# Splitting one weight load of a streamed expert layer into five transfers

## The reference

```
def _expert_choice_ffn(h, w_router, w_gate, w_up, w_down):
    ...
    def expert(args):
        xe, wg, wu, wd = args
        a = jnp.einsum('bcd,df->bcf', xe, wg)
        u = jnp.einsum('bcd,df->bcf', xe, wu)
        return jnp.einsum('bcf,fd->bcd', jax.nn.silu(a) * u, wd)

    out = lax.map(expert, (xin, w_gate, w_up, w_down))
    out = out * g[..., None].astype(out.dtype)
    return jnp.zeros_like(h).at[bi, idx].add(out)
```

## Time and profile before

| | |
|---|---|
| median of three runs | 1815.48 us (1813.34 to 1815.5) |
| the profiled execution, its own time | 1813.51 us |
| its span | 1811.5 us |
| TensorE busy | 1350.9 us, 75% of the span |
| VectorE, ScalarE, GpSimd busy | 438.3, 143.5, 36.2 us |
| moved by DMA | 629.34 MB, mean 347 GB/s |
| chain that ended last | DMA 57%, TensorE 40% |

### The profile page before, as it was taken

One profiled execution on the slowest core, in us unless ns is written; L12 is line 12 of the kernel. 1 busy time (PEld: TensorE's weight loads), 2 busy tenths in 40 slices (PEclk: granted clock), 3 DMA queues, 4 the chain that ended last, 5 costly groups with the idle time before them and its releaser, 6 DMA issues.

```text
span 1811.5 us, 22396 instructions
## 1 busy us (share of the span) xinstructions
PE 1350.9 (75%) x10436; PEld 750.2 (41%) x10436; DVE 438.3 (24%) x681; ACT 143.5 (8%) x316; POOL 36.2 (2%) x54
## 2 busy tenths in 40 slices
PE   9999999999999765756656575666656574665665
PEld 7888588848765331312312231322222131221321
DVE  3553333368655101010211101010210101021111
ACT  3200021132221000000000000000000000000001
POOL 1001010000000000000000000000000000000000
PEclk9999999999999877878777877878777887778788
DMA  7425372432399999999999999999999999999996
GB/s 253 141 95 157 101 251 94 148 139 94 132 383 414 432 431 432 433 432 432 432 431 431 433 434 432 431 430 432 435 431 433 431 430 433 433 430 434 431 428 274
DMA packets 50688, 629.34 MB, mean 347 GB/s; under 512 B 3098, under 2 KB 4293, under 8 KB 36772
## 3 DMA queue, kind: packets, MB, share of 16 engines
q1 hardware_dynamic: 47776, 620.01, 81.5%
q0 software_dynamic: 2400, 7.56, 1.5%
q10 hardware_dynamic: 420, 0.34, 0.1%
HBM read 626.79 MB, written 1.11 MB: 347 GB/s over the span
## 4 chain that ended last, share of the span: by engine, by line
DMA 57%; PE 40%; DVE 1%; ACT 1%; issue 0%; POOL 0%; DVEq 0%; SPq 0%; ACTq 0%
DMA arena<-in_w_down 21%; DMA arena<-in_w_gate 18%; DMA arena<-in_w_up 18%; PE psum L907 12%; PE psum L1517 7%; PE psum L1573 4%; PE psum L1277 3%; PE psum L1207 2%; PE psum L910 2%; PE psum L1367 1%; PE psum L913 1%; PE psum L1181 1%; PE psum L1195 1%; PE psum L1279 1%; PE psum L1506 1%; PE psum L1426 0%
## 5 line engine op out<-in xcount | busy, mean ns | idle before, releaser
L1517 PE MATMUL psum<-arena 128*32 128x352 f32 x4096 | 409.4, 565 | 326.0 <-DMA arena<-in_w_up 194.7
L1517 PEld LDWEIGHTS psum<-arena 128*32 128x32 f32 x4096 | 150.7, 132 | 585.0 <-issue 223.4
L1573 PE MATMUL psum<-arena 128*32 128x512 f32 x1408 | 232.0, 774 | 62.4 <-DMA arena<-in_w_down 62.4
L907 PE MATMUL psum<-arena 128*128 128x256 f32 x976 | 222.1, 383 | 1.3 <-ACT arena L611 0.7
L907 PEld LDWEIGHTS psum<-arena 128*128 128x128 f32 x976 | 181.7, 189 | 30.1 <-issue 2.2
L2203 DVE TENSOR_SCALAR arena<-arena 128x704 f32<-128x704 f32 x16 | 12.0, 753 | 654.1 <-ACT arena L856 654.0
L1573 PEld LDWEIGHTS psum<-arena 128*32 128x32 f32 x1408 | 62.6, 134 | 218.4 <-issue 138.5
L2210 DVE TENSOR_TENSOR arena<-psum,arena 128x704 f32<-128x704 f32 x16 | 21.5, 1344 | 303.5 <-PE psum L1517 303.5
L1506 PE MATMUL psum<-arena 128*128 128x32 f32 x512 | 89.5, 347 | 0.8 <-DVE arena L2167 0.8
L1506 PEld LDWEIGHTS psum<-arena 128*128 128x128 f32 x512 | 88.7, 273 | 2.1 <-issue 1.1
L859 ACT ACTIVATE arena<-psum 128x1024 f32<-128x1024 f32 x15 | 15.4, 1024 | 778.1 <-PE psum L1573 778.1
(11 more groups left out here) (385 smaller groups left out, 951.9 us busy)
## 6 DMA issues: line engine op xcount, KB each, us to landing
arena<-in_w_gate SPq DMA_DIRECT2D x32, 5632.0 KB, 46.6
arena<-in_w_up SPq DMA_DIRECT2D x31, 5632.0 KB, 45.2
arena<-in_w_down SPq DMA_DIRECT2D x28, 5632.0 KB, 47.6
arena<-in_w_in SPq DMA_DIRECT2D x24, 2048.0 KB, 8.6
arena<-in_w_down SPq DMA_DIRECT2D x11, 1408.0 KB, 41.0
arena<-in_w_out SPq DMA_DIRECT2D x4, 2048.0 KB, 7.9
arena<-in_w_down SPq DMA_DIRECT2D x2, 2816.0 KB, 15.6
arena<-in_w_up SPq DMA_DIRECT2D x2, 1408.0 KB, 15.6
```

The costliest lines, as they stand in the source:

```text
L907: last = mm(o, block_of(blk)[:, k, c * P:c * P + P], rhs[:, k, :], start=(k == 0), stop=(k == KC - 1))
L1517: last = mm(psum[32 * j:32 * j + CAP, b + n, 0:HALFQ], XC[:, k, :], region(o, HALFQ), start=(k == 0), stop=(k == KC - 1))
L1573: last = mm(psum[32 * g:32 * g + CAP, gate + 1 - n, :], HT[:, i, :], region(spot(pos), 512), start=(i < 4), stop=(i >= FPP - 4))
```

## The change

Transfer number `PARTED`, tenth from the end of the list, is the last four-row transfer. It is issued as five: partitions 0 to 95 as one, and partitions 96 to 127 as four, each of eight partitions in steps of four (96, 100, ... 124; then 97, 101, ...). Each of the five adds 16 to the transfer's semaphore, and TensorE waits for 80 more instead of 16 more.

```
         sizes += [4 * FF] * (6 * E - 8) + [FF] * 7 + [2304, 512]
+        PARTED = len(sizes) - 10
+        assert sizes[PARTED] == 4 * FF
...
             def expert_rows(n):
 
                 pos, size = loads[n]
-                sp.dma_start(region(spot(pos), size), load(pos, size)).then_inc(arrived[n % NA], 16)
+                if n == PARTED:
+                    sp.dma_start(region(spot(pos), size)[0:96, :], load(pos, size)[0:96, :]).then_inc(arrived[n % NA], 16)
+                    for p0 in range(96, 100):
+                        sp.dma_start(region(spot(pos), size)[p0:P:4, :], load(pos, size)[p0:P:4, :]).then_inc(arrived[n % NA], 16)
+                else:
+                    sp.dma_start(region(spot(pos), size), load(pos, size)).then_inc(arrived[n % NA], 16)
...
             def arrive(pos):
 
                 while starts[seen[0]] < pos:
-                    pe.wait_ge(arrived[seen[0] % NA], 16 * (seen[0] // NA + 1))
+                    pe.wait_ge(arrived[seen[0] % NA], 16 * (seen[0] // NA) + (80 if seen[0] == PARTED else 16))
                     seen[0] += 1
```

## The result

| | before | changed |
|---|---|---|
| median | 1815.26 us (4 runs, 1813.34 to 1815.5) | 1845.27 us (4 runs, 1842.82 to 1845.76) |
| ratio | | 1.0166, 95% interval 1.0155 to 1.0178 |
| span of the profiled execution | 1811.5 us | 1843.7 us |

The change makes the kernel 30 us slower. The profiled execution of the kernel before was about 2 us under its median, so between the two profiles the difference is 32 us.

A forecast was written before the change was run, and what follows sets the result against it. The prediction took the last landing of the weight stream to bound the kernel. The places-written term (-1.8 to +2.0 us, middle 0) and small terms of nothing added 0 to 1815.48 us: forecast 1815.5 us, range 1812.2 less 0.4 to 1822.0 us.

The forecast's parts named there:

- What bounds the kernel: Expert part: a weight stream whose last landing, 1798.39 us, sets the end; moving it by x moves the end by x.
- Half of the engines lag the other half: Stream's tail: eight engines end on average at 1789.0 us, the other eight at 1797.8, a lag of 8.8 us.
- code fetches are its cause: In the stream: 51 code packets, some 62 us of engine time, would give 7.8 us each on eight engines alone.
- If those are always the same eight: Parted transfer: if its four small transfers always use the same eight engines, these get 10 rows and the others 6.
- that they might be the early half: Parted transfer: early engines take the extra rows, late ones lose 3.33 us; whole gain -3.33 us, 1812.2 us, chance 0.18.
- all late, the rival: Parted transfer: the eight engines taking the small transfers are the late ones; +3.33 us, 1818.8 us or more; chance 0.14.
- the reading of rows 7: Rates with 64-partition loads, 241 to 252 GB/s, taken as one half's intake, against its 217 in the 433 GB/s stream.
- the term for the places written to: Partitions 96 to 127, written by early engines beside late ones: last landing moves -1.8 to +2.0 us, middle 0 taken.
- Collisions in the 96-partition transfer: Late engines' six rows share their places with others' at 0.58 to 0.5 rate; +3.9 to +6.7 us; chance 0.21.
- Small terms: Four more SyncE issues (1.3 us, covered), four more completions and the wait for 80: together nothing.
- the rate near 1765 us: Sign for the forecast: below 430 GB/s at full share, engines waiting for each other, plateau on to about 1798 us.
- The sign given for collisions: Sign on TensorE's timeline: its products would start at 1776 us or later.

The follow-up runs named there:

- four loads by columns: Kernel before, with the PARTED transfer issued as four loads of 128 partitions x 2816 columns on the same semaphore: 1814.28 us, ratio 1.0000.
- 96 and 32 partitions: Changed kernel, with partitions 96 to 127 as one transfer instead of four of eight, beside 0 to 95; complete: 1842.03 us, ratio 1.0155.
- eight in steps of four from 0: Changed kernel, with only four transfers of eight partitions, moved to 0 to 31 in steps of four; partitions 32 to 127 left out: 1805.8 us.
- the run with partitions 4 to 35: Changed kernel, with only four transfers of eight partitions, moved to 4 to 35 in steps of four; the rest left out: 1815.6 us.
- blocks of eight: Changed kernel, with only partitions 0 to 31 loaded, as four blocks of eight neighbours; 32 to 127 left out: 1824.55 us.
- those of four: Changed kernel, with only four transfers of four partitions, 0 to 15 in steps of four; the rest left out: 1800.29 us.

## Why the prediction was wrong

- **What bounds the kernel** held. The last landing and the end moved by the same 32.2 us; TensorE waited for DMA at every group, and its margin (could it follow?) was never tested, since landings only got later.
- **Half of the engines lag the other half** held, and the run with four loads by columns shows it again in its own stretch of the tail:

```profile
1791.00:1797.00 6.00, 4.79 (x22) 0.77 (x16) 0.00 (x0) 0.00 (x0) 0.00 (x0) 0.74 0.50 211
```

  That code fetches are its cause fits in time and roughly in size: the lag between the halves grows with them, from 0.5 us at 510 us to 3.2 at 1005 and 8.8 at the end. The 51 packets took 53.9 us together, not the 62 read from a rounded share, so 6.7 us on eight engines and not 7.8. No run here took them away, and that they go to the late eight alone is not shown.
- **"If those are always the same eight"** held; **that they might be the early half** (or all late, the rival) did not: six early, two late. Had nothing else happened, the two late ones with ten rows would have ended 3.3 us later than before. The largest possible gain was never -3.33 us but a loss of 3.33. With 96 and 32 partitions, where each engine would have eight rows if all sixteen share both, the cost is 27.8 us, against 30.0 us for the change: 2.2 us less, the right side and about the size.
- **The step that failed** is the reading of rows 7, and with it the term for the places written to. I took 241 to 252 GB/s as what *a half of the partitions* takes in, left the other half its own rate, and charged the meetings to the engines that meet. The rows said something harder: they are what *the whole core* moves while several engines meet in others' partitions. Loads to 64 partitions are such a case (with four rows on each of 16 engines, half of the engines must be guests), and beside them the queue with 128 partitions was slow as well. Only where a single pair met did the local price hold (3.32 us a row, 0.85 to 0.89 us a packet for its host, the others at 0.42). The term "-1.8 to +2.0 us" measured +27 to +30 us (30.0 less the 3.3 of the two rows, or the 29.7 of the missing bytes).
- **Collisions in the 96-partition transfer** was the rival with the right place and the wrong price. I priced one engine's six rows (+3.9 to +6.7 us); alone that transfer costs 19.7 us over the kernel before and, set against six rows an engine at full rate (-3.3 us), 23 us, because the delay is everybody's and lasts for both groups in turn: the early engines pass through it some 9 us before the late ones, and each slows the other.
- **Small terms** held: issues and completions cost nothing (four loads by columns). One slip in the sums: the collisions' upper end is 1822.2 us, and the range has 1822.0.
- What I named as signs was half right: the rate near 1765 us fell below 430 GB/s at full share, as I wrote for the forecast; that it would be 182 GB/s over 1750 to 1770 us, and stay low until the late engines were through, was not in any case. The sign given for collisions, products at 1776 us or later, is the one that came (1804.53).

## What to carry to other kernels

Cut a stream of loads by columns and leave each transfer all 128 partitions: that was free here, while a cut by partitions cost up to 30 us for 5.6 MB, also for transfers around it that nobody touched. A cut by partitions kept the full rate only where each engine stayed in its own (eight in steps of four from 0). When a stretch shows the DMA engines fully busy at about half the usual rate, ask first whether some load in flight has fewer than 128 partitions, and whether its engines meet the owners of the partitions. If several do, count its price as half of the time that it is under way, for everybody, with early and late engines counted one after the other; if one does, count only its pair. A share that falls in steps at a stream's end (0.50, then 0.13) tells how many engines are left, and so whether a transfer of few rows went where one hoped.

## What the runs showed of the hardware

- **Two guests that meet owners slow all, one slows its own pair.** With two engines left at rows of others' partitions, all sixteen moved 208 GB/s (1792 to 1800 us of the changed kernel) instead of 423 to 433, every packet at twice its length. With one left the rate was 406 GB/s (1803 to 1804 us there), and 387 in 1765 to 1772 us of the run with partitions 4 to 35. (A guest is an engine that writes another's partitions.) The Trainium skill (SBUF — State Buffer, "Door 1: The DMA port swizzle") gives a limit for each port of 27.2 GB/s, and 218 GB/s for 64 partitions. As a limit of a port it leaves the fourteen engines outside a pair at their rate, and with one pair the trace agrees; with two pairs it would leave twelve, which the trace contradicts. As a rate for the core, 218 is close to the 182 to 226 GB/s measured over most of the slow stretches, though not to the 117 where both groups of engines were in the parted transfer. Why the others are held back stays open: the trace does not number engines or ports. Nor is the step from one to two a law: with several guests in one group (blocks of eight, 1771 to 1773 us) the others' packets took 1.3 times their length.
- **Which engines a small transfer takes is fixed**: the four transfers of eight partitions loaded the same eight engines (two of them late), those of four the same four, as the tails show: with other engines each time there would be no two stragglers at 0.13.
- **The lag between two halves of the engines** (8.8 us at the end) does not follow the halves of the partitions. The eight engines that own partitions 0 to 63, by the Trainium skill's split, include six early and two late.
